# Six buffers for modulation tiles, and the weight sums of the second layer's Strassen steps on GpSimd

## What is computed

```python
for l in range(DEPTH_2):                                  # DEPTH_2 = 2
    mod = (silu(c) @ w_ada[l] + b_ada[l])                 # 6 * 1024 numbers; the same for c_ctx
    sh1, sc1, g1, sh2, sc2, g2 = split(mod, 6)
    mem = context_memory(modulate(xc, ...), p)            # layer 0: also a full update of xc
    x = post(x, latent_mixer(modulate(x, sh1, sc1), mem, cos, sin, p), g1, ln1_g[l], ln1_b[l])
    x = post(x, ffn(modulate(x, sh2, sc2), p), g2, ln2_g[l], ln2_b[l])

def ffn(h, p):
    return (silu(h @ w_ff_gate) * (h @ w_ff_up)) @ w_ff_down     # 1024 -> 2816 -> 1024
```

## Time and profile before

| | |
|---|---|
| time, median of 3 runs | 3348.33 us (3346.26 to 3360.38) |
| time of the profiled execution | 3341.68 us |
| its span, first to last instruction | 3339.9 us |
| PE busy | 3123.9 us (94%), mean granted clock 0.982 |
| DVE busy | 1599.2 us (48%) |
| ACT busy | 664.3 us (20%) |
| POOL busy | 52.2 us (2%) |
| DMA | 363.09 MB, mean 109 GB/s |

### The profile page before, as it was taken

One profiled execution on the slowest core, in us unless ns is written; L12 is line 12 of the kernel. 1 busy time (PEld: TensorE's weight loads), 2 busy tenths in 40 slices (PEclk: granted clock), 3 DMA queues, 4 the chain that ended last, 5 costly groups with the idle time before them and its releaser, 6 DMA issues. The chain is left out here.

```text
span 3339.9 us, 40779 instructions
## 1 busy us (share of the span) xinstructions
PE 3123.9 (94%) x13492; PEld 2273.2 (68%) x13492; DVE 1599.2 (48%) x3314; ACT 664.3 (20%) x1621; POOL 52.2 (2%) x101
## 2 busy tenths in 40 slices
PE   9998999989969899999999989999989999998998
PEld 8887888878855555644444438885446667887887
DVE  4455136646663356755554144441134556754551
ACT  3334110000003333300002022110043331022111
POOL 0000001100010000000000000000000000000000
PEclk9999999999989999999999999999999999999999
DMA  5233357746641111112221112222211122433443
GB/s 185 96 134 119 114 177 267 267 148 229 245 176 51 40 40 53 52 49 78 79 75 57 69 44 76 82 94 82 78 41 53 54 76 94 152 107 113 149 150 104
DMA packets 104878, 363.09 MB, mean 109 GB/s; under 512 B 11376, under 2 KB 17520, under 8 KB 104688
## 3 DMA queue, kind: packets, MB, share of 16 engines
q1 hardware_dynamic: 90720, 310.92, 26.9%
q0 software_dynamic: 14096, 51.39, 4.3%
HBM read 361.21 MB, written 1.05 MB: 108 GB/s over the span
## 5 line engine op out<-in xcount | busy, mean ns | idle before, releaser
L499 PE MATMUL bank<-H,W 128*128 128x256 f32 (+1 forms) x3600 | 988.3, 432 | 13.3 <-DVEq L276 10.8
L499 PEld LDWEIGHTS bank<-H,W 128*128 128x128 f32 x3600 | 687.2, 192 | 295.4 <-issue 217.9
L499 PE MATMUL bank<-YG,W 128*128 128x256 f32 (+1 forms) x2336 | 679.1, 449 | 13.4 <-ACTq L276 11.1
L499 PEld LDWEIGHTS bank<-YG,W 128*128 128x128 f32 x2336 | 445.2, 191 | 236.2 <-issue 193.5
L730 PE MATMUL bank<-MX,SQ 128*128 128x256 f32 (+1 forms) x1056 | 184.9, 332 | 17.6 <-DVE SQ L1725 15.3
L730 PEld LDWEIGHTS bank<-MX,SQ 128*128 128x128 f32 x1056 | 162.8, 192 | 38.1 <-issue 10.2
L1983 DVE SCALAR_TENSOR_TENSOR YG<-WORK,PR,YG 128x512 f32 (+1 forms) x240 | 147.0, 612 | 0.0
L1660 DVE TENSOR_SCALAR WORK<-bank,MOD 128x256 f32<-128x256 f32 x48 | 21.8, 481 | 260.3 <-PE bank L499 260.2
L1020 ACT ACT_TABLE_LOAD x20 | 25.7, 1283 | 588.8 <-DVEq L276 587.6
L1983 DVE SCALAR_TENSOR_TENSOR WORK<-WORK,PR 128x512 f32<-128x512 f32 (+1 forms) x224 | 137.2, 612 | 0.0
L1590 DVE SCALAR_TENSOR_TENSOR WORK<-WORK,MX 128x1024 f32<-128x1024 f32 x96 | 117.5, 1223 | 38.3 <-DMA WORK<-ada 32.7
(11 more groups left out here) (295 smaller groups left out, 3385.8 us busy)
## 6 DMA issues: line engine op xcount, KB each, us to landing
W<-stream SPq DMA_DIRECT2D x556, 512.0 KB, 3.3
WORK<-ada POOLq DMA_DIRECT2D x96, 512.0 KB, 3.9
W<-stream SPq DMA_DIRECT2D x24, 384.0 KB, 3.2
W<-stream SPq DMA_DIRECT2D x16, 128.0 KB, 2.5
CN<-consts SPq DMA_DIRECT2D x1, 1984.0 KB, 15.5
X<-x_in SPq DMA_DIRECT2D x2, 512.0 KB, 5.1
MX<-mem_in SPq DMA_DIRECT2D x1, 1024.0 KB, 10.7
X<-ctx_in SPq DMA_DIRECT2D x1, 1024.0 KB, 11.3
```

Of the source, the lines that this page charges most:

```text
L499: m = pe.matmul(out_ap, W[u][:, c, :], src[:, c, cols], start=first and c == 0, stop=last and c == k - 1)
```

## The change

1. `ada_w` has six buffers in place of two (two more in `SQ`, one more in `WORK`, one in the unused end of `YG`), and the table `ADA_TURNS` tells which buffers and how many tiles a turn of each phase uses. The tiles are spread anew: `merge1` 6 in each turn as before (buffers 0 to 5), `out1` 3 in each of 2 turns (0 to 2), `up1` 2 in each turn as before (0 and 1), head of `down1` 4 (2 to 5), `down1` 4 in each turn (0 to 3), two behind each addition: 48 + 6 + 22 + 4 + 16 = 96.
2. In `up2` of layer 1 the weight sums are no longer on DVE. GpSimd makes them in a loop of its own with 11 turns, behind all its transfers. Waits and events are those that DVE had. In layer 0 they stay on DVE.
3. Some semaphores of phases far apart now share one name (`attn_normed` and `ffn_normed` become `chunk_normed`, `left_hidden` becomes `acc_taken`, and the like), and `cond_sig` lies in `SQ`.

```diff
-ADA_SLOTS = 2
-ADA_MERGE, ADA_UP, ADA_DOWN = 6, 2, 6
+ADA_SLOTS = 6
+ADA_TURNS = {"merge1": (8, 0, 6), "out1": (2, 0, 3), "up1": (11, 0, 2), "before_down1": (1, 2, 4), "down1": (4, 0, 4)}
...
-        ada_w = [work(4096 + u * 1024, 4, S) for u in range(ADA_SLOTS)]
+        ada_w = [work(4096, 4, S), work(5120, 4, S), SQ[:, 0:4, CTX], SQ[:, 4:8, CTX], work(3072, 4, S),
+                 YG[:, FT * T2:FT * T2 + D].rearrange("p (c t) -> p c t", c=4)]
...
-            def ada_tile(n, k):
-
-                u = k % ADA_SLOTS
-                dve.wait_ge(tally.sem("ada_done"), n + (k + 1))
-                dve.wait_ge(tally.sem(f"ada_loaded{u}"), (n + (k - u)) * 8 + 16)
+            def ada_tile(name, turn, k):
+
+                first, loads, _, slot, count = ADA_AT[name]
+                u = slot + k
+                dve.wait_ge(tally.sem("ada_done"), turn * count + (first + k + 1))
+                dve.wait_ge(tally.sem(f"ada_loaded{u}"), turn * 16 + (loads[u] + 1) * 16)
...
             def out1(s):
...
                     dve.tensor_tensor(t, t, bank[u][:, 0:S], ALU.add).then_inc(*s.tick(f"added{u}"))
+                    if u < 3:
+                        ada_tile("out1", s.turn, u)
+                ada_keep("out1", s.turn)
...
             def ada_before_down1(layer):
 
-                n = ADA_TILES + ADA_UP * 11
-                for k in range(2):
-                    ada_tile(n, k)
-                ada_keep(n, 1, n - ADA_TILES, 2, 8 + 11 + 1)
+                for k in range(4):
+                    ada_tile("before_down1", 0, k)
+                ada_keep("before_down1", 0)
...
             def down1(s):
...
                     dve.tensor_tensor(t, t, bank[j][:, 0:S], ALU.add).then_inc(*s.tick(f"added{j}"))
-                    for k in range(3 * j, 3 * j + 3):
-                        ada_tile(n, k)
+                    for k in range(2 * j, 2 * j + 2):
+                        ada_tile("down1", s.turn, k)
...
                 for j in range(2):
-                    sum_weights(j)
+                    if not s.layer:
+                        sum_weights(j)
                     first(j)
...
-            for n in range(LAYERS * ADA_TILES):
-                if n >= ADA_SLOTS:
-                    pool.wait_ge(tally.sem("ada_done"), n - ADA_SLOTS + 2)
-                pool.dma_start(ada_w[n % ADA_SLOTS], ada[n].rearrange("p (c t) -> p c t", c=4))\
-                    .then_inc(tally.sem(f"ada_loaded{n % ADA_SLOTS}"), 16)
+            last = {}
+            for n, u in enumerate(ADA_SLOT_OF):
+                if u in last:
+                    pool.wait_ge(tally.sem("ada_done"), last[u] + 2)
+                pool.dma_start(ada_w[u], ada[n].rearrange("p (c t) -> p c t", c=4))\
+                    .then_inc(tally.sem(f"ada_loaded{u}"), 16)
+                last[u] = n
+
+            def sum_weights(s, j):
+                a, b = W[j], W[2 + j]
+                made = f"w_summed{j}"
+                pool.wait_ge(*s.done(f"loaded{j}"))
+                pool.wait_ge(*s.done(f"loaded{2 + j}"))
+                pool.wait_ge(*s.before(f"c12{j}"))
+                pool.tensor_tensor(w_sum[j][0], b[:, EVEN, :], b[:, ODD, :], ALU.add).then_inc(*s.tick(made))
+                pool.tensor_tensor(w_sum[j][2], a[:, EVEN, :], b[:, EVEN, :], ALU.add).then_inc(*s.tick(made))
+                pool.wait_ge(*s.done(made))
+                pool.tensor_tensor(w_sum[j][1], w_sum[j][0], a[:, EVEN, :], ALU.add).then_inc(*s.tick(made))
+                pool.wait_ge(*s.done(made, 2))
+                pool.tensor_tensor(w_sum[j][3], w_sum[j][1], a[:, ODD, :], ALU.add).then_inc(*s.tick(made))
+
+            n = plan.index(("up2", 1, 11, [KC * P] * 4))
+            pool.wait_ge(tally.sem("phase_done"), WORKERS * n)
+            with pool.Fori(0, plan[n][2]) as turn:
+                for j in range(2):
+                    sum_weights(Step(tally, plan, n, turn), j)
```

More of the change, by code:

```diff
@@ L47, with ada_plan @@
 ADA_TILES = 48
-ADA_SLOTS = 2
-ADA_MERGE, ADA_UP, ADA_DOWN = 6, 2, 6
+ADA_SLOTS = 6
+ADA_TURNS = {"merge1": (8, 0, 6), "out1": (2, 0, 3), "up1": (11, 0, 2), "before_down1": (1, 2, 4), "down1": (4, 0, 4)}
+def ada_plan():
+    first, loads, kept, out, slots = 0, [0] * ADA_SLOTS, 0, {}, []
+    for name, (turns, slot, count) in ADA_TURNS.items():
+        out[name] = (first, list(loads), kept, slot, count)
+        slots += list(range(slot, slot + count)) * turns
+        loads = [n + (turns if slot <= u < slot + count else 0) for u, n in enumerate(loads)]
+        first, kept = first + turns * count, kept + turns
+    return out, slots, kept
+ADA_AT, ADA_SLOT_OF, ADA_KEPT = ada_plan()
 def first_column(layer):
@@ L201, in program @@
         small = sb("small", 64)
-        MODS = [sb(f"MOD{l}", ADA_TILES, 2) for l in range(LAYERS)]
-        ada_sums = sb("ada_sums", ADA_MERGE, 2)
+        MOD = sb("MOD", LAYERS * ADA_TILES, 2)
+        MODS = [MOD[:, l * ADA_TILES:(l + 1) * ADA_TILES, :] for l in range(LAYERS)]
+        ada_sums = sb("ada_sums", ADA_SLOTS, 2)
         tile_sum = sb("tile_sum", T2)
@@ L735, in up2 @@
                     pe.wait_ge(*s.before(f"first_taken{j}"))
-                    pe.wait_ge(*s.before(f"left_hidden{j}"))
+                    pe.wait_ge(*s.before(f"acc_taken{j}"))
                     pe.wait_ge(*s.done(f"loaded{j}"))
@@ L899, in gla @@
                 project(s, 1, bank[1][:, :], slice(0, T2))
-                pe.wait_ge(*s.before("gla_rstd"))
+                pe.wait_ge(*s.before("head_rstd"))
                 project(s, 2, bank[0][:, 0:n], slice(c0, T2))
@@ L1058, in forget @@
             def forget(s):
-                act.wait_ge(*s.done("forget_logits"))
+                act.wait_ge(*s.done("logits"))
                 y, e = small_f[0:FW, 0, :], small_f[0:FW, 1, :]
@@ L1593, in ada_tile, with ada_keep @@
                                          accum_out=ada_sums[:, k, 1:2]).then_inc(tally.sem("ada_done"), 1)
-            def ada_keep(n, layer, tile, count, kept):
-                dve.wait_ge(tally.sem("ada_done"), n + (count + 1))
-                dve.tensor_copy(MODS[layer][:, bass.ds(tile, count), :], ada_sums[:, 0:count, :])\
+            def ada_keep(name, turn):
+                first, _, kept, _, count = ADA_AT[name]
+                dve.wait_ge(tally.sem("ada_done"), turn * count + (first + count + 1))
+                dve.tensor_copy(MOD[:, bass.ds(turn * count + first, count), :], ada_sums[:, 0:count, :])\
                    .then_inc(tally.sem("ada_kept"), 1)
-                dve.wait_ge(tally.sem("ada_kept"), kept)
+                dve.wait_ge(tally.sem("ada_kept"), turn + (kept + 1))
             def merge(s, count, cols):
@@ L1615, in merge @@
                     for k in ((0, 1), (2,), (3, 4), (5,))[n]:
-                        ada_tile(s.turn * ADA_MERGE, k)
-                ada_keep(s.turn * ADA_MERGE, 0, s.turn * ADA_MERGE, ADA_MERGE, s.turn + 1)
+                        ada_tile("merge1", s.turn, k)
+                ada_keep("merge1", s.turn)
             def merge1(s):
@@ L1703, in up1 @@
                        .then_inc(*s.tick(f"hidden{j}"))
-                    ada_tile(s.turn * ADA_UP + ADA_TILES, j)
-                ada_keep(s.turn * ADA_UP + ADA_TILES, 1, s.turn * ADA_UP, ADA_UP, s.turn + (8 + 1))
+                    ada_tile("up1", s.turn, j)
+                ada_keep("up1", s.turn)
             def sum_hidden(layer):
@@ L1952, in gla @@
                 silu(1)
-                dve.wait_ge(*s.done("gla_rstd"))
+                dve.wait_ge(*s.done("head_rstd"))
                 for e in range(2):
```

36 lines of the change are left out of this document (17 added, 19 removed).

## The result

| | before | after |
|---|---|---|
| median of the runs, us | 3347.3 (3345.29 to 3360.38, 4 runs) | 3391.69 (3383.68 to 3393.27, 4 runs) |
| ratio, 95% interval | | 1.0119 (1.0089 to 1.015) |
| profiled execution, us | 3341.68 | 3392.12 |
| `up2` of layer 1, us | 165.9 | 219.6 |
| additions on GpSimd | none | 88, of 1.27 to 1.29 us (means of the four groups) |

The changed kernel is slower by 1.2%, or 44 us. (The median before differs a little from that of the prediction, since one run more was made beside the changed kernel.)

A forecast was written before the change was run, and what follows sets the result against it. PE was taken to bound the kernel, busy 3123.9 of 3339.9 us. Tiles -15.2, sums on GpSimd +34 and clock +4 gave +23 us on 3348.33, so 3371 us (+0.7%), range 3335 to 3402.

The forecast's parts named there:

- Tiles, -15.2: Modulation tiles in `merge1` to `down1`: `ln_mixer` starts at 966.7, not 982.30; -15.2 us in sum.
- The +0.4 behind `out1`: End of `out1`: the copy of the sums comes behind the last addition, before the norm's ACT work; +0.4 us with waits.
- Duration of a sum, 1.22 us: `up2` of layer 1: GpSimd reads its two operands one after the other, so one weight sum takes 1.22 us.
- Where `second(1)` starts, +10.3: `up2` of layer 1: seven GpSimd sums put `second(1)` at +10.3 us from the turn's first matmul, 3.5 us later.
- break-even point: `up2` of layer 1: the sum duration t where 7t + 1.8 = 6.8, at t = 0.72 us.
- First turn, +1.1: First turn of `up2` in layer 1: all tiles loaded, seven sums end at 3091.7 against 3090.41; +1.1 us.
- The clock, +4: `up2` of layer 1: PE's clock falls behind idle gaps in every fourth turn; +4 us, possible 0 to 15.
- a granted clock under 0.9 in this phase: `up2` of layer 1: a granted clock below 0.9 there would show the forecast wrong.
- That GpSimd adds as fast as DVE, or nearly: Sums in `up2`, layer 1: t below 0.8 gives 3328 us, chance 0.08; t near 0.95 gives 3347, chance 0.17.
- That the six buffers do not work: End of `down1`: DVE is still late, the tiles are worth 0, and the time is 3386 us; chance 0.03.
- A clock that falls in each turn: `up2` of layer 1: clock at 1.2 GHz each time with t = 1.22, 3382 us; chance 0.11 shared with t = 1.76.
- three passes: `up2` of layer 1: GpSimd cannot write while reading, a sum takes 1.76 us, 3409 us; chance 0.11 shared with low clock.

The follow-up runs named there:

- the first experiment: The changed kernel with the weight sums of layer 1 back on DVE, so only the modulation tiles changed: 3331.71 us, ratio 0.9962 to the kernel before.

## Why the prediction was right, and where its sizes were off

- **Direction and mechanism held.** PE bounds the kernel, DVE's sums were cheap because they were short, and the seven sums in front of `second(1)` set the turn. Each part alone moved the time as forecast, down with the first and up with the second. The total is nearly twice the forecast (44 us for 23).
- **Tiles, -15.2.** Measured -15.9 in the profile, and 13 us by the medians of the tiles alone. `ln_mixer` came at 966.44, forecast 966.7; that it is so close is partly luck, since in the five profiles with these tiles it lies between 962.77 and 967.28, by the clock behind the gaps in front of it. The gap of 5.99 us was the forecast 6, and the 16 matmuls behind it took 9.89 us; behind the long gap they took 8.64 before and 9.69 with the sums alone, so the clock cost about the same. The +0.4 behind `out1` was 0.15 in the gap (2.76 for 2.61). The clock fell behind it, 5.20 us for 3.69, but not because of those 0.15: behind 2.76 us it stayed up with the tiles alone (3.69), and behind 2.62 it fell in the kernel with the sums alone, which has the old code there (5.08).
- **Duration of a sum, 1.22 us.** The start of one to the start of the next is 1.22 in most pairs and 1.34 where the sum reads the one just made (3159.69 to 3161.03); seven take 8.71 us, and 8.54 were forecast. The step was right, and the half columns bear out its reason as far as a time can: from 512 to 256 elements the spacing falls from 1.22 to 0.68 us, by the same 0.54 that the prediction had taken for one more pass over 512. That the operands are read one after the other is still inferred. The estimate from the 1.96-fold of the Trainium skill (GPSIMD Engine Reference, Performance versus the Vector engine) was 1.34; the record shows 1283 against 686 ns, 1.87-fold.
- **Where `second(1)` starts, +10.3.** It was +10.89 on average over the ten later turns. I had GpSimd start at +1.7; it started at +2.22 in the turn shown, held by a transfer of weights, and near +2.0 on average (10.89 less 8.71 for the seven sums and 0.15 to PE's start). Behind it 0.48 us were won in the turns whose clock was up, for a forecast 0.2. In all 3.57 us in a turn for 3.3: 35.7 for 33. These two misses work against each other in the break-even point too: by the rows after, a turn is as long as before at (6.84 + 0.48 - 2.03 - 0.15) / 7 = 0.73 us for a sum, start to start, for the forecast 0.72, and the half columns, with 4.93 / 7 = 0.70, lie just below.
- **First turn, +1.1.** It was +5.05: `second(1)` came 3.37 us later, the 32 matmuls behind it took 5.97 us for 3.81, which is 2.16 of clock, and 0.48 were won behind them. Here a mechanism was missing from the sum: all transfers are long done, so GpSimd's sums and DVE's sums of the activations run at the same time, and lock each other out. PE's `second(0)` then waits for the last sum of the activations, not for GpSimd. The timeline of that turn:

```profile
3077.23 1.65 DVE L1735 SCALAR_TENSOR_TENSOR MX<-MX,H 128x512 f32<-128x512 f32 x1
3078.30 1.70 POOL L2050 TENSOR_TENSOR SQ<-W 128x512 f32<-128x512 f32 x1
...
3078.80 1.75 DVE L1736 TENSOR_TENSOR MX<-H 128x512 f32<-128x512 f32 x1
...
3082.35 2.07 PE L746 MATMUL bank<-MX,SQ 128*128 128x128 f32 x8 [2.86 <-DVE MX L1738]
```

- **The clock, +4.** This is the term that failed. "I take a fall in every fourth turn" was read from one gap of 2.61 us that left the clock alone. It fell in all 11 turns: in 9 of them behind `second(1)`'s gap or still low there, 1.41 to 2.16 us each, together 15.1 us, the upper end of the bound of 0 to 15, and in two at `second(0)`, where it cost nothing. The row that I went by was one draw: in nine profiles the gap behind `out1`, of 2.61 to 2.76 us, was followed by a fall in five. The same holds for the premise that a gap of 3.73 us lowers the clock: behind 3.75 it stayed at 1.00 in one profile of five. A turn has two gaps, of about 2.2 and 2.6 us, with 2.5 us of work between them, where my row had one. What makes the clock fall in each turn stays open: that the pair is the cause was not tried, and in the two turns with the early fall only the first of the pair had gone by. The stretches of the turn shown, one microsecond each, from 3166 on:

```profile
3166.00:3167.00 1.00, 0.90 (x7) 0.93 (x8) 0.00 (x0) 0.00 (x0) 0.97 (x1) 0.89 0.33 131
3167.00:3168.00 1.00, 1.00 (x7) 1.00 (x7) 0.00 (x0) 0.28 (x1) 0.30 (x1) 0.50 0.00 0
```

The clock falls from 2.4 to 1.2 GHz (1.00 to 0.50) shortly after PE has begun again. The experiment with the filled gaps gave this term back. I had named a granted clock under 0.9 in this phase as a sign that the forecast is wrong; it was 0.88, and this part was wrong.

- **Sum.** 35.7 in ten turns, 15.1 of clock in all eleven and 5.05 - 2.16 = 2.9 in the first: 53.7 us in `up2` for a forecast 38. With the tiles that is +37.8, or a ratio of 1.0113, inside the measured interval. Of the 12.6 us in the stretches of equal work, the 3.3 behind `up2` are no part of the change: the same stretch takes 94.3 us both with the sums alone and with the filled gaps, which has both parts of the change, and 98.0 with the tiles ahead of the last addition, which has no sums on GpSimd. The 9.3 between `ln_mixer` and `up2` stay open. That stretch took 2097.4 and 2099.7 us in the two profiles with the old tiles, and 2102.5 to 2107.3 in the six with new tiles and `up2` of layer 0 as before, so some 3 us or more might belong to the tiles. But both of the former are of executions faster than the median of their kernel, the time lies in the granted clock, and the medians are 44 us apart, not 50.
- **Rivals.** That GpSimd adds as fast as DVE, or nearly, fell with 1.28 us; the run on half the columns shows that at 0.74 it would have come out so. That the six buffers do not work fell with the first experiment. "A clock that falls in each turn" came true, with a cost in 9 turns of 11; it had 3382 us for the measured 3391.69, and I had given it, together with three passes, a chance of 0.11.

## What to carry to other kernels

Work goes to an idle engine only if its duration there still fits in front of the consumer that waits: here the break-even was at about 0.73 us for each of seven sums in a row, GpSimd needs 1.24 and DVE 0.69, and DVE was not short of time. Price a gap of 2 us and more that comes back in each turn on PE at the low clock, even if one such gap in a trace left the clock alone, and look for a change that takes the gap away: the order of DVE's own work (tiles ahead of the last addition, the fourth sums last) took the ratio from 0.9962 to 0.9898, where the other engine cost 1.7%.

## What the runs showed that I had not expected

- A two-input f32 addition on GpSimd takes 1283 ns for 128x512 and 740 ns for 128x256 by its rows, and 1.22 and 0.68 us from one start to the next: 2.1 ns for an element in a partition, and 0.1 to 0.2 us fixed. DVE takes 686 ns for 128x512.
- GpSimd and DVE additions exclude each other: when they meet in the first turn of the changed kernel they take 1.60 to 1.75 us, where they have 1.27 and 0.69 alone.
- The same code runs at other clocks from run to run, and the length of a gap of 2 to 4 us alone did not decide it. Behind `out1` the clock stayed up in one profile with 2.61 us and in three with 2.76, and fell in one with 2.62 and in four with 2.76. Single profiles differ by up to 10 us in 2100 us of equal work, with granted clocks of 0.98 and 0.99.
- Matmuls that compute nothing, put in front of a wait of PE, made the changed kernel 14 us (by the ratios) to 20 us (by the medians) faster.
